# Seams between the stages of a two-layer kernel: what runs first, and how finely sums are read out

## What is computed

```python
# first layer, end
x = x + jnp.einsum('bse,ed->bsd', mixed, w_out[l])
h2 = _rmsnorm(x, ffn_norm_w[l])
g, u = jnp.split(jnp.einsum('bsd,df->bsf', h2, w_gate_up[l]), 2, axis=-1)
x = x + jnp.einsum('bsf,fd->bsd', jax.nn.silu(g) * u, w_down[l])   # d_ff = 5632
# second layer, end: the same with a gain gt2 for each column
x = x + gt2 * ((jax.nn.silu(gate) * up) @ w_ffn_out)
```

## Time and profile before

| | before |
|---|---|
| median of 3 runs (lowest, highest) | 2783.59 us (2783.5, 2786.26) |
| the profiled execution: time | 2782.42 us |
| its span | 2780.6 us |
| PE busy in the span | 2687.8 us, 97% |
| DVE busy | 1754.0 us, 63% |
| ACT busy | 1298.3 us, 47% |
| mean granted clock of PE, share of full speed | 0.986 |
| DMA, mean over the span | 209 GB/s |

### The profile page before, as it was taken

The page is one execution under the profiler, slowest core; times in us unless marked ns, Lnnn a source line. Parts: engine busy times, 40 slices in busy tenths (PEclk is TensorE's granted clock), DMA queues, the critical chain, the costliest instruction groups (busy, mean ns, idle before and its releaser), DMA issues.

```text
span 2780.6 us, 34710 instructions
## 1 busy us (share of the span) xinstructions
PE 2687.8 (97%) x12421; PEld 2220.3 (80%) x12421; DVE 1754.0 (63%) x2045; ACT 1298.3 (47%) x1512; POOL 3.2 (0%) x9
## 2 busy tenths in 40 slices
PE   8999999999999999999799999999899999999998
PEld 6888888778888887877577888888688888887777
DVE  5778668476767677776675554575476644445555
ACT  5555544354434343433555566644344444434433
POOL 0000000000000000000000000000000000000000
PEclk9999999999999999999899999999899999999999
DMA  7766455588788887876555455555488766554544
GB/s 250 246 199 194 144 154 177 184 272 279 270 273 279 275 283 269 280 248 216 156 191 160 143 163 162 187 185 179 139 272 279 235 196 188 183 187 154 192 160 160
DMA packets 302073, 581.44 MB, mean 209 GB/s; under 512 B 19916, under 2 KB 20292, under 8 KB 301716
## 3 DMA queue, kind: packets, MB, share of 16 engines
q1 hardware_dynamic: 300896, 576.34, 64.1%
q10 hardware_dynamic: 740, 2.27, 0.2%
q0 software_dynamic: 336, 1.46, 0.2%
HBM read 577.89 MB, written 2.10 MB: 209 GB/s over the span
## 4 chain that ended last, share of the span: by engine, by line
PE 92%; DVE 5%; ACT 2%; issue 1%; DMA 0%; ACTq 0%; SPq 0%; DVEq 0%
PE acc L341 29%; PE acc L342 28%; PE acc L343 28%; DVE lo L330 2%; PE ex L979 1%; PE aux L1000 1%; PE tp L1354 1%; PE aux L539 1%; DVE op_lo L468 0%; ACT hi L324 0%; ACT xn L409 0%; PE tp L448 0%; ACT stage L460 0%; PE aux L1979 0%; DVE op_hi L467 0%
## 5 line engine op out<-in xcount | busy, mean ns | idle before, releaser
L330 DVE TENSOR_TENSOR lo<-raw,hi 128x1024 fp32r<-128x1024 f32 x895 | 1077.3, 1223 | 501.9 <-ACT hi L324 476.5
L324 ACT ACTIVATE hi<-raw 128x1024 fp32r<-128x1024 f32 x895 | 926.8, 1055 | 667.4 <-PE acc L343 535.7
L341 PE MATMUL acc<-hi,op_hi 128*128 128x512 f32 x2752 | 1090.7, 396 | 25.1 <-DVE lo L330 23.8
L343 PE MATMUL acc<-hi,op_lo 128*128 128x512 f32 x2752 | 1076.4, 391 | 0.0
L342 PE MATMUL acc<-lo,op_hi 128*128 128x512 f32 x2752 | 1075.6, 391 | 0.0
L341 PEld LDWEIGHTS acc<-hi,op_hi 128*128 128x128 f32 x2752 | 518.6, 188 | 138.2 <-issue 27.8
L343 PEld LDWEIGHTS acc<-hi,op_lo 128*128 128x128 f32 x2752 | 518.3, 188 | 109.7
L342 PEld LDWEIGHTS acc<-lo,op_hi 128*128 128x128 f32 x2752 | 519.0, 189 | 102.7 <-issue 0.2
L341 PE MATMUL acc<-hi,f_hi 128*128 128x512 f32 x704 | 283.2, 402 | 19.1 <-issue 11.9
L342 PE MATMUL acc<-lo,f_hi 128*128 128x512 f32 x704 | 281.5, 400 | 0.0
L343 PE MATMUL acc<-hi,f_lo 128*128 128x512 f32 x704 | 280.9, 399 | 0.0
(11 more groups left out here) (291 smaller groups left out, 1410.7 us busy)
## 6 DMA issues: line engine op xcount, KB each, us to landing
raw<-w_in SPq DMA_DIRECT2D x257, 512.0 KB, 3.9
ada_ring<-w_ada SPq DMA_DIRECT2D x192, 512.0 KB, 5.2
raw<-w_gate_up SPq DMA_DIRECT2D x176, 512.0 KB, 4.9
raw<-w_ffn_in SPq DMA_DIRECT2D x176, 512.0 KB, 4.6
raw<-w_down SPq DMA_DIRECT2D x88, 512.0 KB, 5.6
raw<-w_ffn_out SPq DMA_DIRECT2D x88, 512.0 KB, 4.4
raw<-w_out SPq DMA_DIRECT2D x64, 512.0 KB, 4.4
raw<-w_proj_mla SPq DMA_DIRECT2D x16, 512.0 KB, 4.2
```

The costliest lines, as they stand in the source:

```text
L324: A.activation(hi[:, k, :, 0:n], raw[:, k, :, 0:n], ACT.Copy).then_inc(hi_ready, 1)
L330: V.tensor_tensor(lo[:, k, :, 0:n], raw[:, k, :, 0:n], hi[:, k, :, 0:n].bitcast(F32), ALU.subtract).then_inc(lo_ready, 1)
L341: T.matmul(dst, lh, hi[:, k, kk, 0:n], start=first and kk == 0, stop=False)
L343: mm = T.matmul(dst, ll, hi[:, k, kk, 0:n], start=False, stop=last and kk == CK - 1)
```

## The change

1. `dve_out1` returns its last readout, and DVE runs it after the first weight chunk of gu1 (`begun`). ACT's wait for all readouts of out1 moves from piece 2 of the feed to piece 4.
2. The last pair's product, transposes and copies leave the end of gu1 and gu2. DVE does the product in step 1 of the down projection (between its two chunks), PE the transposes after step 0, ACT the copies in step 2. Each even step waits only for the part of `hid` that it reads. The `w_ada` work of dn1 starts two steps later.
3. Each accumulator is read out by itself: `dn_done` waits for that accumulator's last chunk (43 or 44 of the half), PE waits for the accumulator it is about to start, and DVE does `readout(0, 0)` after the second chunk of step 22, `readout(0, 1)` after the first of step 23. The readouts of the second half follow the last step, the first of them one chunk earlier than before.
4. dn2's steps are written out instead of looped, and the row of gains is made later: DVE in step 4, PE after step 5, ACT after step 7.
5. The last block of the output is multiplied, added and stored by token tile: half instructions, and two stores of 256 KB in place of one of 512 KB.

The computed values are the same. The diff, cut to its core:

```diff
-            readout(1, 1)
+            return lambda: readout(1, 1)
...
+        def act_turn(act, n, i):
+
+            f = ff[n]
+            act.wait_ge(f["tr"], i * 2 + 2)
+            hs = hid[:, ds(i * 4, 4), :].rearrange("p k n -> p (k n)")
+            for j in range(2):
+                A.activation(hs[:, j * NB:(j + 1) * NB], tp[:, j], ACT.Copy).then_inc(f["ev"], 1)
...
+                        if begun and not later(i) and m == 0 and k == 0:
+                            begun()
...
-            product(10)
-            if n == 1:
-                dve_ada_keep(dve, A_DN1 - 1, 0)
+
+        def pe_turn(pe, n, i):
...
-            turn(10)
...
+            for j in range(STEPS):
+                q, kc = dn_at(j)
+                for m in range(2):
+                    c0 = (2 * q + m) * NB
+                    sp_chunk(sp, CH[f"dn{n}"] + 2 * j + m, 0, 4, w[kc][:, :, c0:c0 + NB])
+                s = j - 2
+                if n == 1 and 0 <= s < DN1_ADA:
+                    sp_ada(sp, A_DN1 + s // 8, 0, s % 8, ada_ring2)
...
-                            if q and u == 1 and m == 0 and not later(i):
-                                readout(0, 0)
-                                readout(0, 1)
...
+        def act_dn(act, n):
+            f, c0 = ff[n], CH[f"dn{n}"]
+            for j in range(STEPS):
+                q, kc = dn_at(j)
+                if j >= 2:
+                    act.wait_ge(chunk_used, c0 + 2 * j - 2)
+                if q == 0 and kc % 2 == 0:
+                    act.wait_ge(f["ev"], kc + 2)
+                A.activation(f_hi[:, j % 2], hid[:, 2 * kc:2 * kc + 2, :], ACT.Copy).then_inc(f["sp"], 1)
+                for m in range(2):
+                    act_chunk(act, c0 + 2 * j + m, 0, 4)
+                    if j == 2 and m == 0:
+                        act_turn(act, n, 10)
+                if n == 2 and j == 7:
+                    act_row(act, 1)
...
+        def dve_dn(dve, cd, n, lo_done, readout, roots=None):
+            f, c0 = ff[n], CH[f"dn{n}"]
+            for j in range(STEPS):
+                q, kc = dn_at(j)
+                dve.wait_ge(f["sp"], j + 1)
+                V.tensor_tensor(f_lo[:, j % 2], hid[:, 2 * kc:2 * kc + 2, :], f_hi[:, j % 2].bitcast(F32), ALU.subtract).then_inc(lo_done, 1)
+                for m in range(2):
+                    dve_chunk(dve, c0 + 2 * j + m, 0, 4)
+                    if j == 1 and m == 0:
+                        dve_product(dve, n, 10, roots)
+                    if (j, m) in ((22, 1), (23, 0)):
+                        readout(0, 1 - m)
+                if n == 2 and j == 4:
+                    dve.wait_ge(f["tr"], 22)
+                    dve_row(dve, 80)
+                if n == 1 and j == 1:
+                    dve_ada_keep(dve, A_DN1 - 1, 0)
+                s = j - 2
+                if n == 1 and s >= 0:
+                    if s < DN1_ADA:
+                        dve_ada(dve, cd, A_DN1 + s // 8, 0, s % 8, ada_ring2)
+                    if s >= 8 and s % 8 == 1:
+                        dve_ada_keep(dve, A_DN1 + s // 8 - 1, 0)
             readout(1, 0)
             readout(1, 1)
...
+        def pe_dn(pe, n, lo_done):
+            f, c0, b = ff[n], CH[f"dn{n}"], BL[f"dn{n}"]
+            for j in range(STEPS):
+                q, kc = dn_at(j)
+                pe.wait_ge(lo_done, j + 1)
                 for m in range(2):
-                    pe_acc_wait(pe, BL[name] + 2 * q + m, 0, 2)
-
-                def four(i, first=None, last=None):
-                    for u in range(2):
-                        pe.wait_ge(lo_done, i * 2 + 22 * q + u + 1)
-                        for m in range(2):
-                            c = CH[name] + 44 * q + 2 * u + m
-                            pe_chunk(pe, c, i, 4, acc[:, (BL[name] + m) % 2], 0,
-                                     first and u == 0, last and u == 1, left=(f_hi[:, u], f_lo[:, u]))
-                        if beside and q == 0 and u == 0 and first:
-                            beside()
-                        if n == 1:
-                            j = 2 * (11 * q + i) + u
-                            if j < DN1_ADA and j % 8 == 7:
-                                pe_ada(pe, A_DN1 + j // 8, 0)
-                if n == 1:
-                    for i in range(11):
-                        four(i, i == 0, i == 10)
-                    continue
-                four(0, True, False)
-                with pe.Fori(1, 10) as i:
-                    four(i, False, False)
-                four(10, False, True)
-
-        def dn_done(dve, name, q):
-            dve.wait_ge(chunk_used, CH[name] + 44 * (q + 1))
+                    if kc == 0:
+                        pe_acc_wait(pe, b + 2 * q + m, 0, 2)
+                    pe_chunk(pe, c0 + 2 * j + m, 0, 4, acc[:, (b + m) % 2], 0, kc == 0, kc == 21, left=(f_hi[:, j % 2], f_lo[:, j % 2]))
+                if j == 0:
+                    pe_turn(pe, n, 10)
+                if n == 2 and j == 5:
+                    pe.wait_ge(f["ev"], 22)
+                    pe_row(pe, 1)
+                s = j - 2
+                if n == 1 and 0 <= s < DN1_ADA and s % 8 == 7:
+                    pe_ada(pe, A_DN1 + s // 8, 0)
+
+        def dn_done(dve, name, q, m):
+            dve.wait_ge(chunk_used, CH[name] + 44 * q + 43 + m)
...
+            for j in range(3):
                 sp.wait_ge(added, 4 + j + 1)
                 sp.dma_start(out[0][:, j * NB:(j + 1) * NB].rearrange("(t p) n -> p t n", p=P), x[:, :, j * NB:(j + 1) * NB]).then_inc(s_out, 16)
-            sp.wait_ge(s_out, 64)
+            for t in range(TT):
+                sp.wait_ge(added, 8 + t)
+                sp.dma_start(out[0][t * P:(t + 1) * P, 3 * NB:], x[:, t, 3 * NB:]).then_inc(s_out, 16)
+            sp.wait_ge(s_out, 80)
...
-                if k == 2:
+                if k == 4:
                     wait_free(act, "out1")
...
+            last = dve_out1(dve, cd)
+            dve_gu(dve, cd, 1, dve_fed(dve, cd, "ffn1", 8), 1, last)
+            dve_dn(dve, cd, 1, dn_lo[1], readout_dn1(dve), 1)
...
+                    if name == "dn2" and j == 3:
+                        for t in range(TT):
+                            V.tensor_tensor(gt_tmp[:, t], acc[:, p, t], gt_row[:, c], ALU.mult).then_inc(tail, 1)
+                            dve.wait_ge(tail, t + 1)
+                            V.tensor_tensor(x[:, t, c], x[:, t, c], gt_tmp[:, t], ALU.add).then_inc(added, 1)
+                        return
...
-            pe.wait_ge(ff[2]["ev"], 22)
-            pe_dn(pe, 2, dn_lo[2], lambda: pe_row(pe, 1))
+            pe_dn(pe, 2, dn_lo[2])
```

More of the change, by code:

```diff
@@ L1257, in act_gu @@
             p0 = BL[name] % 2
[L1259 to L1264, removed]
+            evac = lambda i: act_turn(act, n, i)
             def pair(i):
@@ L1293, in act_gu, with dve_product, dve_gu @@
             turns(act, 11, pair)
-            evac(10)
-        def dve_gu(dve, cd, n, feed, roots=None):
+        def dve_product(dve, n, i, roots=None):
             name, f = f"gu{n}", ff[n]
             p1 = (BL[name] + 1) % 2
[L1300 to L1313, removed]
+            block_done(dve, name, i, 1)
+            dve.wait_ge(f["g"], i + 1)
+            if later(i):
+                dve.wait_ge(f["tr"], i * 2)
+            if roots:
+                for t in range(TT):
+                    ins = V.scalar_tensor_tensor(out=f_a[:, t], in0=acc[:, p1, t], scalar=small[:, 3, t:t + 1],
+                                                 in1=f_g[:, t], op0=ALU.mult, op1=ALU.mult)
+            else:
+                ins = V.tensor_tensor(f_a[:], f_g[:], acc[:, p1], ALU.mult)
+            ins.then_inc(f["a"], 1)
+            dve.wait_ge(f["a"], i + 1)
+            dve.sem_inc(acc_free[p1])
+        def dve_gu(dve, cd, n, feed, roots=None, begun=None):
+            name, f = f"gu{n}", ff[n]
+            product = lambda i: dve_product(dve, n, i, roots)
             ada_at = dve_ada_at(dve, cd, A_GU1 if n == 1 else A_GU2, ada_ring2, before=False)
@@ L1380, in build_program, with dn_at @@
         DN1_ADA = 5 * 8
+        def dn_at(j):
+            return j // 22, j % 22
         def sp_dn(sp, n, w):
[L1383 to L1393 removed]
@@ L1395, in w_slice @@
[L1395 to L1415, removed]
-                        beside()
-                turns(act, 11, four)
@@ L1419, in dve_dn @@
-        def dve_dn(dve, cd, n, lo_done, readout, beside=None):
-            name, f = f"dn{n}", ff[n]
-            for q in range(2):
-                def four(i):
-                    for u in range(2):
-                        dve.wait_ge(f["sp"], i * 2 + 22 * q + u + 1)
-                        V.tensor_tensor(f_lo[:, u], hid[:, ds(i * 4 + 2 * u, 2), :], f_hi[:, u].bitcast(F32), ALU.subtract).then_inc(lo_done, 1)
-                        for m in range(2):
-                            dve_chunk(dve, CH[name] + 44 * q + 2 * u + m, i, 4)
-                            if beside and q == 0 and not later(i) and u == 0 and m == 1:
```

(12 more changed lines are left out.)

65 lines of the change are left out of this document (24 added, 41 removed).

## The result

| | before | after |
|---|---|---|
| median (lowest, highest) | 2784.74 us (2783.5, 2786.26), 4 runs | 2746.12 us (2745.31, 2748.3), 4 runs |
| ratio, 95% interval | | 0.9862 [0.9845, 0.9879] |
| profiled execution, span | 2780.6 us | 2744.2 us |
| granted clock, mean | 0.986 | 0.991 |

The forecast was 2747.2 us, with 2742.5 to 2756 for 8 in 10. The span shrank by 36.4 us, the sum of the forecast to the tenth. The medians lie further apart than the spans, 38.6 us; the profiled execution of the kernel before, from which every term was read, was one of its faster ones, as the experiments show at the first seam.

A forecast was written before the change was run, and what follows sets the result against it. PE bounds the kernel (92% of the chain), with its waits taken to stand at the seams between stages. Terms 3.5 + 6.7 + 8.0 + 6.2 + 8.3 + 1.15 + 2.6 = 36.4 us: 2783.6 becomes 2747.2 us; own range 2743.5 to 2751, 8 in 10 2742.5 to 2756.

The forecast's parts named there:

- out1 to gu1: Start of gu1: its first chunk starts at out1's last matmul instead of behind the last readout; 3.5 us, bounds 2.5 and 3.6.
- gu1 to dn1: Start of dn1: PE does step 0 instead of waiting for the last pair's product, copies and split; 6.7 us, lower bound 5.
- gu2 to dn2: Start of dn2: the same waiting and slow clock go, the row of gains moves later; 8.0 us, lower bound 6.5.
- The middles: Step 22 of dn1 and dn2: separate readouts save net 6.2 and 8.3 us, leaving PE waits of 1.4 and 1.3 us.
- End of dn1: Behind dn1's last matmul: the first of two additions moves before it, so layer two's norm starts 1.15 us earlier.
- End of the kernel: Behind the last matmul: 2.9 us of DVE instructions instead of 5.0, last store 0.5 us shorter; sum 2.6 us.
- Written-out dn2: Steps of dn2 as straight code instead of a loop: costed at nothing, steps staying at 5.58 us.
- the first three rivals: Fallen clock, incomplete head start and hand-back before gu1: 32% together, at 2750.7 to 2752.6 us, or 2758 if together.
- the fallen clock: Rival, middles of dn1 and dn2: remaining stalls bring back 1.2 GHz, slow matmuls keep 2.4 and 3.0 us; 2752.6 us; 12%.
- the incomplete head start: Rival, both ends of gu: the product comes late and PE waits for accumulator 1, about 2 us each; 2751 us; 10%.
- the hand-back: Rival, early gu1: weight loads set the pace, so starting gu1 earlier gains nothing; 2750.7 us; 10%.
- the slower case: Rival, dn2: fetching straight-code instructions costs PE more than 0.41 us per chunk; 2800 us at 0.6 us; 3%.

The follow-up runs named there:

- the second measurement: The changed kernel, nothing altered, measured once more on one chip beside another version: 2744.85 us, ratio to before 0.9859.
- when undone: Changed kernel with the last pair's product, transposes and copies put back ahead of step 0 of both down projections: 2762.13 us, ratio to before 0.992.
- the undone ends: Changed kernel with out1's last readout again ahead of gu1's first chunk and the last output block added and stored whole: 2752.23 us, ratio to before 0.9884.
- the filled gaps: Kernel before, with 5 (dn1) and 6 (dn2) idle matmuls of constants ahead of PE's wait in the middles: 2779.12 us, ratio to before 0.9982.
- the inserted ones of 3.8 and 5.05 us: Changed kernel with extra DVE instructions ahead of accumulator 1's readout, dn1/dn2: one/two, span 2750.0 us; two/one, 2748.6; three/three, 2758.8.

## Why the prediction was right, point by point

- *out1 to gu1*, 3.5 us: in the trace the wait of PE at 581.65 moved to 578.16, so 3.5 for that pair of executions. As a typical price it is too small, since in three of four profiled executions the clock falls behind that gap and the seam then costs about 5.1. The step that failed is the reading of one execution's clock as the rule. The medians point the same way: they fell by 38.6 us (40.0 in the second measurement) against the 36.4 forecast. That the missing 1.6 us at this seam are a part of it is likely and not shown, since the other executions have no trace.
- *gu1 to dn1* and *gu2 to dn2*, 6.7 and 8.0 us: 6.7 and 7.95, and again 6.7 and 8.2 when undone. No new wait of PE appeared behind the head start.
- *The middles*, 6.2 and 8.3 us: 6.2 and 8.2. The order of DVE's queue, written out instruction by instruction with durations of the earlier trace rows, gave both the accumulator that would be late and by how much (1.4 and 1.3 us, measured 1.27 both). In dn2, 8.2 is not a constant: 6.9 in another execution with fewer slow matmuls.
- *End of dn1*, 1.15 us: 1.0.
- *End of the kernel*, 2.6 us: 2.5. The sum was right because it counted from T to the end over all edits. But four halves instead of four whole instructions mixes two edits, and the expectation for the undone ends gave the whole to the store by token tile. It is worth 0.1; the split by accumulator is worth the rest. Halving the store saved 0.34 us, less than the 0.5 taken. The estimate from the Trainium skill's page "DMA: Bandwidth & Descriptors", section "Anatomy of one DMA — SWDGE (gpsimd) path", was 0.6 us; that section is about transfers issued by GpSimd, and these stores are issued by SyncE. Its point, that a part of the time does not shrink with the bytes, fits the 3.16 us that became 2.82 here.
- *Written-out dn2*, nothing: nothing.
- *The sum*: the terms above give 36.1 us where 36.4 were forecast; the 0.4 us in the second half of dn2, less 0.1 us elsewhere, close the difference. That is luck.
- *Where the recorded working is off*: the first three rivals coming together add up to 2760.1 us, not 2758; the lower bounds of the terms add up to 26.3 us, which is 2757 and not the 2751 of the own range. PE's waits for `lo` do not stand at the seams alone: 6.6 us of the 34.7 are four waits within layer two's attention, and they are still there.
- *Rivals*: the fallen clock has the right price (2.2 and 2.8 us by the filled gaps) and did not come at 1.27 us; the incomplete head start did not come, with 0.34 us of DVE's idle time ahead of the product; the hand-back and the slower case are refuted. That no load was late in the first steps is seen in every execution, but no kernel here made one late.

What stays open: the two medians of the changed kernel differ by 1.3 us (2746.12, 2744.85), the start of the kernel up to the last readout of out1 takes 543.5 to 544.8 us in the profiled executions for no reason that is known, and the stretch of layer two between its norms, the same code in every kernel, differs by up to 2.8 us. The clock explains most of the last, as the end of this text shows; which executions get it cannot be told from these traces. The 1.0 us at the end of dn1 was not undone by itself.

## What to carry to other kernels

Look for the cost of a PE-bound kernel at its seams, and price each as its gap plus the slow matmuls behind it, from more than one execution, since the clock does not fall in all of them; then write down the other engine's queue in order, instruction by instruction, and find what is late next, since that is where the remaining pause (here 1.27 us, twice) and the next edit are. Give the work that frees an accumulator its place ahead of work that is only needed later. Cut an output into smaller pieces only if more instructions behind the last matmul do not eat what the smaller last store gives.

## What the runs showed of the hardware that was not expected

The clock's fall depends on more than a pause's length. With PE at 2.4 GHz, gaps of 3.6 us ahead of gu1 left the clock at 1.00 in one profiled execution (the one in the earlier trace rows) and brought it to 1.2 GHz in three others; in the middles, pauses of 2.5 us did it once in two, those of 1.27 and 2.0 us in none of ten, the inserted ones of 3.8 and 5.05 us in all of four. Two pairs of waits in layer two, 1.3 and 2.3 us and some 15 us later 1.1 and 1.8 us, the same in every kernel here, belong to this. Where the clock falls behind the second pair, PE's chain reads

```profile
1471.33 0.60 PE acc L341
1471.93 0.43 PE acc L342
1472.35 0.43 PE acc L343
```

(the kernel with both accumulators read out together, 9 matmuls at 1.2 GHz). The stretch of layer two between its two norms takes 667.6 to 667.8 us in the four executions where the clock fell behind both pairs, and 664.9 to 665.9 us in the ten where it fell behind one or neither. So a step that no edit touches moves by 2 us between executions, more than some of the edits here are worth, and a difference of that size is to be read from stretches of the trace and not from two spans. The Trainium skill, page "TensorE: Matmul & The Clock Gate", section "What's actually happening", has the monitor run free of the kernel, so that the point of transition varies. The gaps of 3.6 us, one at 1.00 and three with a fall to 0.50, fit that; no run here shows the monitor itself.
